# Eight query tiles of a head pair in another order: long and short ones in turn

## The reference, cut to what matters

```python
def causal_attention(q, k, v):
    b, s, h, d = q.shape
    nb = s // Q_BLOCK                      # 8 blocks of 128 queries
    scale = 1.0 / math.sqrt(d)
    ...
    def one_block(args):
        q_blk, blk = args
        sc = jnp.einsum('bqhd,bkhd->bhqk', q_blk, k,
                        preferred_element_type=jnp.float32) * scale
        mask = k_pos[None, :] <= q_pos[:, None]
        sc = jnp.where(mask[None, None], sc, -jnp.inf)
        p = jax.nn.softmax(sc, axis=-1).astype(v.dtype)
        return jnp.einsum('bhqk,bkhd->bqhd', p, v)
```

## Time and profile before

| what | value |
|---|---|
| three runs | 3191.34, 3192.62, 3193.46 us |
| profiled execution, from first to last instruction (span) | 3191.1 us |
| instructions in it | 49353 |
| TensorE busy | 3143.4 us, 99% of the span |
| VectorE busy | 1513.3 us, 47% |
| ScalarE busy | 1215.6 us, 38% |
| third attention | from about 2480 to about 2772 us of the span |

### The profile page before, as it was taken

One profiled execution on the slowest core, in us unless ns is written; L12 is line 12 of the kernel. 1 busy time (PEld: TensorE's weight loads), 2 busy tenths in 40 slices (PEclk: granted clock), 3 DMA queues, 4 the chain that ended last, 5 costly groups with the idle time before them and its releaser, 6 DMA issues.

```text
span 3191.1 us, 49353 instructions
## 1 busy us (share of the span) xinstructions
PE 3143.4 (99%) x18948; PEld 2674.9 (84%) x18948; DVE 1513.3 (47%) x3186; ACT 1215.6 (38%) x2410; POOL 565.1 (18%) x818
## 2 busy tenths in 40 slices
PE   7999999999999999999999999999999999999999
PEld 7988889999999888888888888888977777687777
DVE  6657673343354233344432333335344565753775
ACT  5446565444444122132111121124433555622452
POOL 3423334353450000000000000000101110022141
PEclk9999999999999999999999999999999999999999
DMA  5010101111113121130111111113210000212012
GB/s 202 34 47 21 34 21 47 48 54 51 44 51 103 51 75 50 50 139 14 66 42 52 53 40 53 53 53 111 77 36 27 15 28 14 97 57 89 27 60 100
DMA packets 48315, 182.44 MB, mean 57 GB/s; under 512 B 14480, under 2 KB 18704, under 8 KB 35280
## 3 DMA queue, kind: packets, MB, share of 16 engines
q1 hardware_dynamic: 48080, 179.28, 16.2%
HBM read 159.54 MB, written 19.46 MB: 56 GB/s over the span
## 4 chain that ended last, share of the span: by engine, by line
PE 94%; DVE 3%; ACT 2%; issue 1%; DMA 0%; POOL 0%; DVEq 0%; SPq 0%; POOLq 0%; ACTq 0%
PE ps L2108 75%; PE ps L2148 7%; PE ps L2156 3%; PE ps L2114 2%; PE ps L2163 2%; PE ps L2179 2%; PE ps L2171 1%; PE ps L2182 1%; PE ps L2199 1%; DVE wlo L2371 0%; DVE qk L2479 0%; DVE xsc L2443 0%; DVE mPT L2524 0%; DVE mE L2493 0%; DMA min<-in_mem 0%
## 5 line engine op out<-in xcount | busy, mean ns | idle before, releaser
L2108 PE MATMUL ps<-hhi,whi 128*128 128x512 f32 x1568 | 616.4, 393 | 0.0
L2108 PE MATMUL ps<-hhi,wlo 128*128 128x512 f32 x1568 | 610.9, 390 | 0.0
L2108 PE MATMUL ps<-hlo,whi 128*128 128x512 f32 x1568 | 610.1, 389 | 0.0
L2108 PE MATMUL ps<-whi,hhi 128*128 128x256 f32 (+2 forms) x1920 | 580.4, 302 | 1.3 <-DVE hlo L2573 0.9
L2108 PE MATMUL ps<-whi,hlo 128*128 128x256 f32 (+2 forms) x1920 | 563.7, 294 | 0.0
L2108 PE MATMUL ps<-wlo,hhi 128*128 128x256 f32 (+2 forms) x1920 | 563.5, 293 | 0.0
L2692 POOL TENSOR_SCALAR stats<-stats 128x2 f32<-128x2 f32 (+2 forms) x230 | 60.4, 263 | 1937.9 <-ACT jk L2213 805.0
L2108 PEld LDWEIGHTS ps<-whi,hhi 128*128 128x128 f32 x1920 | 368.3, 192 | 10.9 <-issue 3.2
L2108 PEld LDWEIGHTS ps<-wlo,hhi 128*128 128x128 f32 x1920 | 368.8, 192 | 7.6 <-issue 0.2
L2108 PEld LDWEIGHTS ps<-whi,hlo 128*128 128x128 f32 x1920 | 368.3, 192 | 7.7
L2108 PEld LDWEIGHTS ps<-hhi,wlo 128*128 128x128 f32 x1568 | 294.3, 188 | 62.1
(11 more groups left out here) (351 smaller groups left out, 5198.5 us busy)
## 6 DMA issues: line engine op xcount, KB each, us to landing
raw<-in_W SPq DMA_DIRECT2D x93, 1024.0 KB, 4.9
raw<-in_W SPq DMA_DIRECT2D x24, 768.0 KB, 4.4
orw<-scratch_outs SPq DMA_DIRECT2D x6, 1024.0 KB, 5.4
xin<-in_x SPq DMA_DIRECT2D x8, 512.0 KB, 10.9
bW<-scratch_bw SPq DMA_DIRECT2D x8, 512.0 KB, 3.7
x<-in_x SPq DMA_DIRECT2D x8, 512.0 KB, 7.3
scratch_x<-x SPq DMA_DIRECT2D x8, 512.0 KB, 3.7
x1b<-scratch_x SPq DMA_DIRECT2D x8, 512.0 KB, 7.4
```

The lines of the kernel that those rows point to most:

```text
L2108: x = e.matmul(r.out, a, b, start=(r.start and m == 0), stop=(r.stop and m == n - 1))
```

## The change

The eight query tiles of each head pair are listed in the order 7, 0, 6, 1, 5, 2, 4, 3 in place of 7, 6, 5, 4, 3, 2, 1, 0. No instruction is added or taken away. The filling work stays at its steps, and so do the buffers, the banks, and which engine copies which piece: every tile, long or short, takes an even number of turns of the score banks and of the transposition banks, and so each piece falls on the same bank and the same copying engine as before. What a step holds besides the filling work is another tile.

```diff
         for p in range(6):
             us = []
-            for qt in (7, 6, 5, 4, 3, 2, 1, 0):
+            for qt in (7, 0, 6, 1, 5, 2, 4, 3):
                 def make(s, p=p, qt=qt):
```

## The result

The changed kernel took 3204.72 us (median of four runs, 3203.83 to 3206.54), the kernel before 3192.82 us beside it (four runs, 3191.34 to 3193.46). The ratio is 1.0039, with a 95% interval of 1.0024 to 1.0053: slower by 11.9 us, 1.5 us more than the 10.4 us that were forecast, and inside the range (3204.72 us is 1.7 us above the forecast time of 3203.0). The span of the profiled execution grew from 3191.1 to 3202.2 us.

What follows compares the result with a forecast made beforehand. TensorE, busy 99% of the span, bounds the kernel, so only its idle time and clock count. New waits of 19.1 us against old 8.7 give +10.4 on 3192.6: 3203.0 us, range 3195.5 to 3211.

Steps and rivals of the forecast that it cites:

- The chain: DVE and ACT work from a long unit b's first 512 scored keys to its transpositions: 5.31 to 4.46 us, new order.
- 7b: Unit b of tile 7, followed by tile 0: TensorE waits 1.42 us without filling work, plus 0.17 at its second piece.
- 6b: Unit b of tile 6, followed by tile 1: TensorE waits 1.69 us without filling work, plus 0.04.
- TensorE's work in the same time: TensorE's own work before a long unit b's transpositions: 3.89, 2.98, 3.43 and 3.87 us for tiles 7, 6, 5, 4.
- 5b: Unit b of tile 5, followed by tile 2: TensorE waits 1.13 us without filling work.
- 4b: Unit b of tile 4, followed by tile 3: TensorE waits 0.59 us without filling work.
- rival 2: Small score-bank waits make TensorE reach junctions later; new waits 10 to 14 us, time 3194 to 3198 us; chance 0.12.
- The cover by filling work: Filling items hide part of the junction waits: 9.2 us remain in pairs 0, 2, 4 and 2.0 in pairs 1, 3.
- The old waits: TensorE's waits in the old order, at pair starts and ends, pair 5 and before output projection: 8.7 us, nearly all gone.
- The end: Pipeline emptying with two four-block tiles: waits of 0.9, 1.0 and 0.15 us, sum 2.1 us.
- rival 1: Evening out: DVE and ACT run ahead, only about 2 us of waits at the end remain; 3186 us; chance 0.08.
- Rival 3: TensorE's clock also falls after the stage's longer waits: 5 to 9 us more, 3208 to 3212 us; chance 0.10.

## Why the prediction was right, step by step

**The chain.** Right, and to 0.02 us at 7b and 6b. Two experiments take single links out, each with about the effect that the sum gives it (the short copy, 0.72 us at 7b for a copy of 0.69; the ACT copy, a chain 0.54 us shorter at 7b for a link of 0.63, and a change of releaser). That the late exponential, through what is listed behind it, is the larger part of the price is shown by the version in which no copy of a unit a stands behind it; how much of that is ACT's copy alone and how much DVE's sums is not.

**TensorE's work in the same time.** Right at 7b (3.90 us for 3.89). At the later junctions the sum left out a resource: the two score banks. After a long tile's second unit is scored, the next tile's scores come back to a bank that DVE has not emptied, and TensorE waits 0.27 to 0.48 us before it reaches the transpositions. The forecast's 1.69 at 6b became 0.27 + 1.26, its 1.13 at 5b in pair 5 became 0.37 + 0.61; the missing 0.15 us each is TensorE's own work, which took 3.13 us for 2.98 and 3.56 for 3.43. At 4b the forecast's 0.59 at the transpositions is wholly a score bank wait of 0.48 there. The sum hardly changes, because a wait that is met earlier is taken off the one behind it; the name of the wait does. This was rival 2's mechanism ("small waits for score banks"), and it exists, but it does not bring the total down: new waits of 18.7 us, not 10 to 14.

**The cover by filling work.** The prices at the uncovered and half covered junctions of pairs 0, 2 and 4 hold (1.39 + 0.12 for 1.60, 0.80 for 0.87, 0.48 for 0.59, nothing at 6b), and the moved filling shows that an item there removes the wait. The extra 0.8 us for pair 0 was mis-sized: it waits 1.50 + 0.12 us where the others wait 1.39 + 0.12, so 0.1 us more. For pairs 1 and 3 the forecast of 2.0 us is too low, measured 3.3. The term looked at TensorE's time and one copy only. An item of filling work also has its own inputs from DVE: in pair 1 DVE works from 6b's first piece (2549.80) to the second rotation sum (2556.88) with no pause above 0.2 us, and TensorE's turns wait 0.63 us for it (0.25 in pair 3). And its results are copied by ACT. Two such copies, 1.22 us together, stand between 6b's exponential and the copy that counts, so 6b waits 0.17 and 0.48 us for the forecast 0.14:

```profile
2658.95 1.22 ACT L2244 ACTIVATE mkT<-ps 64x512 f32<-64x512 f32 x2
...
2660.84 0.98 PE L2156 MATMUL ps<-ident,mE 128*128 128x128 f32 x7 [0.32 <-ACT mPT L2261]
```

The 0.80 at 5b is there in both pairs. The two errors nearly cancel (-1.5 and +1.3 us), and that the sum of 19.1 came so near to 18.7 is in this part luck.

**The old waits.** As forecast the 0.6 us waits at the pairs' ends, the waits at the starts and the 0.84 us before the output projection are gone. Two of 0.18 us stay at the first pair's start, where the first tile's pieces follow each other in either order. Their sum was 8.0 us and not 8.7.

**The end.** 0.9, 1.0 and 0.15 us were forecast, 0.87, 1.00 and 0.19 measured.

**The rest of the difference.** 10.4 us were forecast, the stage shows 12.0. The waits account for 10.8; 1.2 us lie in distances each less than 0.1 us above their usual length, and their cause stays open.

**The rivals.** The evening out (rival 1) fell: engines that have time to spare in total still run nothing ahead, as each chain begins with b's own scores. The rule of the Trainium skill (Perfetto Trace Analysis, Optimization Strategy) that interleaving regimes of different contended engines may improve performance is not borne out by this trace: DVE stays at 186 us busy of 303, and what was interleaved were not regimes of throughput but the two sides of a latency chain. In the old order the long tiles covered each other, by the forecast's sums with 4.9 to 6.7 us of TensorE work against chains of 4.3 to 5.1. Rival 3 did not come in the profiled execution: the clock is 1.00 in every window of the stage, through five waits of 1.26 to 1.5 us at transpositions. But this is one execution, and the wait of 1.84 us in the first attention, on which the rival rests, shows how little one tells. It is there in the trace of after too, and the clock did not fall:

```profile
333.73 0.41 PE L2114 MATMUL ps<-ident,qk 128*128 128x128 f32 x2 [1.84 <-DVE qk L2479]
...
333.70:337.20 3.50, 3.47 (x29) 3.33 (x31) 0.00 (x0) 1.44 (x5) 1.02 (x1) 1.00 0.43 108
```

Each fall of this length cost 1.5 to 1.6 us where it came. The four runs of after took 3203.83, 3204.02, 3205.41 and 3206.54 us, at mean granted clocks of 0.999, 0.999, 0.998 and 0.997; the profiled one is the second of them. Where the slower two lost their clock, in this stage or elsewhere, is not shown.

## What to carry to other kernels

When the order of work items is changed in a pipeline where each engine runs its list in order, compare, junction by junction, the relay that starts at an item's first result with the work that TensorE has until it needs the answer; shares of busy time tell nothing of it. Look above all for a small copy that is listed behind a long instruction which itself waits (here 0.60 us of ACT behind an exponential that waits for DVE): giving that copy to the other engine, with DVE's sums moved out of its way, was worth 7.7 us of waits in the new order and 1.2 in the old one. Taking away one wait (by a bank, or by an item moved in between) lets TensorE run on to the next late thing, so price what comes next and not only the place at which the wait shows. And before a gain or loss of one or two microseconds is given to an edit, look at the granted clock in both traces, outside the changed stage too.

## What the runs showed of the hardware

Two kinds of DVE instruction of this stage that read and write only SBUF, the spreading of the reciprocals and the two sums of the rotation, last until a GpSimd instruction that was already running has ended. The spreading of the reciprocals (mO) takes 0.23 us at 2706.78 in the last timeline above; at 2715.63 it takes 1.23 us and ends at 2716.86, right behind GpSimd's splitting of weights, which ends at 2716.78. The rotation's second sum takes 0.42 us beside no GpSimd work and 1.38 us at 2717.76, until 2719.14, behind an end at 2718.86. DVE instructions that read PSUM keep their times inside a GpSimd instruction (0.29 and 0.56 us between 2719.92 and 2721.13, while GpSimd runs from 2719.70 to 2720.97). The reciprocal (0.17 us at 2721.99, inside GpSimd's 2721.72 to 2722.98) keeps its time too, though it also reads and writes only SBUF. The Trainium skill (SBUF — State Buffer, SBUF: two separate sides) says that GpSimd and VectorE share one pair of ports as an exclusive lock, that a VectorE instruction contends for it when it runs in a 2-port mode or has two inputs in SBUF while GpSimd's reads SBUF, and that the later one is blocked for the whole instruction. The trace agrees for the rotation's sums, which have two inputs in SBUF, and for the spreading, with 1.23 for 0.23 us; which mode the spreading runs in no trace shows. In this case it is most of the 1.66 us wait in pair 4 by an estimate from rows: ahead of the turns the spreading took 1.24 us and the two sums 0.83 and 1.37 us in that kernel, 2.4 us more than beside no GpSimd work, while in pairs 0 and 2, where GpSimd's instructions are shorter (0.37 to 0.71 us), the same turns don't wait. No run took GpSimd's work away.
